# A decoder layer on one core: inverse and pair products by chunks of 64, another order of the expert loads, and another last pair

## The reference

```python
# gated DeltaNet, 4 heads, chunks of C = 64 tokens
L = where(strict, einsum("bhncd,bhnmd->bhncm", kb, k) * decay, 0)   # per chunk, C x C
T = triangular_solve(L + eye, eye)                                  # inverse, per chunk
u = T @ vb;  w = T @ (kb * exp(gc))
attn = where(incl, einsum("bhncd,bhnmd->bhncm", q, k) * decay, 0)
...   # a scan over the chunks, forgetting attention, gates, output projection, router
# experts: 32, 4 per token
gu = xb @ w_gate_up[e] + b_gate_up[e]                # 1024 x 2048 weights
act = (clip(up) + 1) * (gate * sigmoid(1.702 * gate))
y = act @ w_down[e] + b_down[e]                      # 1024 x 1024 weights
x = x + gt2 * sum of y by gates;  return rms_norm(x, g_final)
```

## Time and profile before

| | us |
|---|---|
| three runs | 1253.33, 1255.08, 1256.19 |
| median | 1255.08 |
| the profiled execution | 1258.74 |
| its span | 1256.7 |
| PE busy | 1152.5 (92%) |
| DVE, ACT, POOL busy | 322.5, 185.2, 106.0 |
| mean rate of all transfers | 370 GB/s |

### The profile page before, as it was taken

One profiled execution on the slowest core, in us unless ns is written; L12 is line 12 of the kernel. 1 busy time (PEld: TensorE's weight loads), 2 busy tenths in 40 slices (PEclk: granted clock), 3 DMA queues, 4 the chain that ended last, 5 costly groups with the idle time before them and its releaser, 6 DMA issues.

```text
span 1256.7 us, 14765 instructions
## 1 busy us (share of the span) xinstructions
PE 1152.5 (92%) x6083; PEld 601.5 (48%) x6083; DVE 322.5 (26%) x674; ACT 185.2 (15%) x316; POOL 106.0 (8%) x50
## 2 busy tenths in 40 slices
PE   4999999999999999998988989898999999999995
PEld 2999799778634434333333333333333333343431
DVE  1633554132232222212221212122121222222112
ACT  2475244100301000000000000000000010000001
POOL 0764343020000000000000000000000000000000
PEclk9999999999999999999999999999999999999998
DMA  9972763398789999999999999999999999999994
GB/s 350 340 231 90 231 217 101 102 414 371 291 363 424 428 428 429 429 428 428 429 428 428 430 427 429 430 427 429 429 428 430 428 428 421 386 429 429 428 426 176
DMA packets 62268, 464.67 MB, mean 370 GB/s; under 512 B 8437, under 2 KB 31098, under 8 KB 34586
## 3 DMA queue, kind: packets, MB, share of 16 engines
q1 hardware_dynamic: 60968, 462.13, 89.6%
q10 hardware_dynamic: 1218, 1.93, 0.5%
q0 software_dynamic: 48, 0.13, 0.0%
HBM read 463.13 MB, written 1.05 MB: 369 GB/s over the span
## 4 chain that ended last, share of the span: by engine, by line
PE 67%; DMA 26%; issue 3%; ACT 2%; DVE 1%; ACTq 0%; SPq 0%; DVEq 0%
PE ps L438 65%; DMA ring<-in_w_down_dram 22%; DMA ring<-in_w_gate_up_dram 3%; PE ps L871 1%; ACT kept L1195 1%; DMA ring<-in_w_in_dram 1%; DMA ring<-in_g_onorm_dram 1%; PE ps L893 0%; PE ps L446 0%; ACT w_hi L1003 0%; DVE ring L1662 0%; ACT ring L986 0%; DVE kept L1326 0%; ACT ring L1041 0%; ACT ring L1212 0%
## 5 line engine op out<-in xcount | busy, mean ns | idle before, releaser
L438 PE MATMUL ps<-ring,kept 128*64 128x512 f32 (+1 forms) x3280 | 713.7, 602 | 44.1 <-DMA ring<-in_w_down_dram 32.5
L438 PEld LDWEIGHTS ps<-ring,kept 128*64 128x64 f32 (+1 forms) x3280 | 230.9, 138 | 496.4 <-issue 428.7
L438 PE MATMUL ps<-kept 128*128 128x128 f32 (+5 forms) x744 | 139.2, 350 | 5.5 <-DVE kept L1564 1.6
L1191 ACT ACTIVATE kept<-kept 128x512 f32<-128x512 f32 x32 | 20.2, 630 | 746.3 <-DVE kept L1598 746.3
L1617 DVE TENSOR_TENSOR kept<-ps,kept 64x512 f32<-64x512 f32 x64 | 44.1, 689 | 315.9 <-PE ps L438 314.9
L438 PEld LDWEIGHTS ps<-kept 128*128 128x128 f32 (+2 forms) x744 | 94.1, 192 | 58.7 <-issue 53.2
L1598 DVE TENSOR_SCALAR kept<-ps 128x512 f32<-128x512 f32 x32 | 22.1, 691 | 371.2 <-PE ps L438 371.2
L1674 POOL TENSOR_TENSOR w_lo<-ring,w_hi 128x1024 fp32r<-128x1024 f32 x38 | 91.9, 2435 | 116.7 <-ACT w_hi L1003 116.7
L438 PE MATMUL ps<-ring 128*128 128x128 f32 (+4 forms) x560 | 87.1, 314 | 2.4 <-issue 2.4
L438 PEld LDWEIGHTS ps<-ring 128*128 128x128 f32 (+3 forms) x560 | 78.4, 193 | 11.0 <-issue 6.3
L438 PE MATMUL ps<-hT_hi,w_hi 128*128 128x256 f32 x272 | 78.4, 288 | 0.0
(11 more groups left out here) (227 smaller groups left out, 519.4 us busy)
## 6 DMA issues: line engine op xcount, KB each, us to landing
ring<-in_w_gate_up_dram SPq DMA_DIRECT2D x128, 2048.0 KB, 26.9
ring<-in_w_down_dram SPq DMA_DIRECT2D x63, 2048.0 KB, 23.8
ring<-in_w_ada_dram SPq DMA_DIRECT2D x24, 1024.0 KB, 5.4
ring<-in_w_in_dram SPq DMA_DIRECT2D x22, 1024.0 KB, 11.4
ring<-in_w_out_dram SPq DMA_DIRECT2D x4, 1024.0 KB, 15.7
ring<-in_w_o_fox_dram SPq DMA_DIRECT2D x2, 1024.0 KB, 9.8
ring<-in_w_o_delta_dram SPq DMA_DIRECT2D x2, 1024.0 KB, 12.2
kept<-in_w_down_dram SPq DMA_DIRECT2D x1, 2048.0 KB, 14.1
```

Source lines behind the costliest of these rows:

```text
L438: return pe.matmul(dst, lhsT, rhs, start=start, stop=stop, skip_group_check=True)
L1191: A(sig_a, gate_a, ACT.Sigmoid, scale=ALPHA).then_inc(S("sig_ready"), 1)
```

## The change

Four parts. (1) The pair products, and the products of the inverse but for R and XR of level 1, are done per chunk: for each `t` and `h` two multiplications, one per chunk `r`. In the pair products each has 128 rows, 64 stationary columns and 64 moving ones; in the inverse each is a 64x64 tile on the diagonal of the array by 64 columns. (2) The transposes of the gate weights go from the start of `open_sums` into the first gate_up, ahead of row block 6. (3) Down weights have three places: low halves of even experts in units 16 and 17, low halves of odd ones in `dn_kept` (the place of `early_dn`), high halves of both in units 18 and 19. The order of the loads is `by_place` for pairs 1 to 9, a mixed one for pair `TURN` = 10, `by_need` for 11 to 14. The very first unit of pair 1 comes as two loads of one row block each, the first of which waits for one used row block instead of two. (4) The last pair has both gate_ups ahead of both downs, in its loads and on TensorE. The even expert's transposed activations go to a place of their own (`act_t_last`), VectorE's steps follow (`last_experts`), and the high half of the last down comes as two loads of 1 MB into units 4 and 5.

```diff
-            def load_dn(e, j):
-                src = w_down[0, e, j * 4 * P:(j + 1) * 4 * P, :].rearrange("(p k) n -> p (k n)", k=4)
-                s0 = 16 + 2 * j
-                sp.dma_start(flat[:, s0 * UNIT:(s0 + 2) * UNIT], src).then_inc(expert_chunk_sem(s0), 16)
+            def load_gu_row(e, par, u, k):
+                src = w_gate_up[0, e, u * 2 * P:(u + 1) * 2 * P, :].rearrange("(p k) n -> p k n", k=2)
+                s0 = par * KD + 2 * u
+                sp.dma_start(flat[:, (s0 + k) * UNIT:(s0 + k + 1) * UNIT], src[:, k, :]).then_inc(
+                    expert_chunk_sem(s0), 16)
+            def dn_rows(e, j):
+                return w_down[0, e, j * 4 * P:(j + 1) * 4 * P, :].rearrange("(p k) n -> p (k n)", k=4)
+            def load_dn(e, par, j):
+                if j == 1:
+                    sp.dma_start(flat[:, 18 * UNIT:20 * UNIT], dn_rows(e, 1)).then_inc(S("dn_high_in"), 16)
+                elif par == 0:
+                    sp.dma_start(flat[:, 16 * UNIT:18 * UNIT], dn_rows(e, 0)).then_inc(S("dn_even_in"), 16)
+                else:
+                    sp.dma_start(dn_kept, dn_rows(e, 0)).then_inc(S("dn_odd_in"), 16)
...
-            def next_dn(I, i, par, js=range(2)):
-                for j in js:
-                    sp.wait_ge(S("dn_used"), I * 8 + (par * 4 - 4 + 2 * j + 2))
-                    load_dn(i * 2 + par, j)
+            def next_dn(I, i, par, j):
+                if j == 1:
+                    sp.wait_ge(S("dn_used"), I * 8 + par * 4)
+                else:
+                    sp.wait_ge(S("dn_used"), I * 8 + (par * 4 - 6))
+                load_dn(i * 2 + par, par, j)
+            def by_place(I, i, first_unit_whole=True):
+                if first_unit_whole:
+                    next_gu(I, i, 0)
+                else:
+                    for k in range(2):
+                        sp.wait_ge(S("gu_used"), I * 16 + (k - 15))
+                        load_gu_row(i * 2, 0, 0, k)
+                    next_gu(I, i, 0, range(1, 4))
+                next_dn(I, i, 0, 0)
+                next_dn(I - 1, i - 1, 1, 1)
+                next_gu(I, i, 1)
+                next_dn(I, i, 1, 0)
+                next_dn(I, i, 0, 1)
+            def by_need(I, i):
+                for par in range(2):
+                    next_gu(I, i, par)
+                    for j in range(2):
+                        next_dn(I, i, par, j)
+            def last_by_need(I, i):
+                for par in range(2):
+                    next_gu(I, i, par)
+                for j in range(2):
+                    next_dn(I, i, 0, j)
+                next_dn(I, i, 1, 0)
+                sp.wait_ge(S("gu_used"), I * 16 + 6)
+                rows = w_down[0, i * 2 + 1, 4 * P:8 * P, :].rearrange("(p k) n -> p k n", k=4)
+                for half, sem in enumerate((S("dn_last_in0"), S("dn_last_in1"))):
+                    at = 4 * UNIT + half * UNIT
+                    sp.dma_start(flat[:, at:at + UNIT].rearrange("p (k n) -> p k n", k=2),
+                                 rows[:, 2 * half:2 * half + 2, :]).then_inc(sem, 16)
             def load_round(I0, first):
-                if not first:
+                if first:
+                    by_place(1, 1, first_unit_whole=False)
+                else:
+                    sp.wait_ge(S("dn_used"), I0 * 8)
                     next_gu(I0, 0, 0)
-                    next_dn(I0, 0, 0)
+                    next_dn(I0, 0, 0, 0)
+                    next_dn(I0, 0, 0, 1)
                     next_gu(I0, 0, 1)
-                if first:
-                    next_gu(I0 + 1, 1, 0)
-                    next_dn(I0, 0, 1, range(1, 2))
-                    next_gu(I0 + 1, 1, 1)
-                    next_dn(I0 + 1, 1, 0)
-                with sp.Fori(2 if first else 1, PAIRS - 3) as i:
-                    next_gu(I0 + i, i, 0)
-                    next_dn(I0 + (i - 1), i - 1, 1)
-                    next_gu(I0 + i, i, 1)
-                    next_dn(I0 + i, i, 0)
-                i = PAIRS - 3
-                next_gu(I0 + i, i, 0, range(1))
-                next_dn(I0 + (i - 1), i - 1, 1)
-                next_gu(I0 + i, i, 0, range(1, 4))
-                next_dn(I0 + i, i, 0)
-                next_gu(I0 + i, i, 1)
-                next_dn(I0 + i, i, 1)
-                for i in (PAIRS - 2, PAIRS - 1):
-                    for par in range(2):
-                        next_gu(I0 + i, i, par)
-                        next_dn(I0 + i, i, par)
+                    next_dn(I0, 0, 1, 0)
+                with sp.Fori(2 if first else 1, TURN) as i:
+                    by_place(I0 + i, i)
+                next_gu(I0 + TURN, TURN, 0)
+                next_dn(I0 + TURN, TURN, 0, 0)
+                next_dn(I0 + (TURN - 1), TURN - 1, 1, 1)
+                next_gu(I0 + TURN, TURN, 1, range(0, 2))
+                next_dn(I0 + TURN, TURN, 0, 1)
+                next_gu(I0 + TURN, TURN, 1, range(2, 4))
+                next_dn(I0 + TURN, TURN, 1, 0)
+                next_dn(I0 + TURN, TURN, 1, 1)
+                with sp.Fori(TURN + 1, PAIRS - 1) as i:
+                    by_need(I0 + i, i)
+                last_by_need(I0 + (PAIRS - 1), PAIRS - 1)
...
+            def chunk_products(banks, a, b):
+                for t in range(TT):
+                    for h in range(H):
+                        for r in range(2):
+                            rows = slice(r * CH, r * CH + CH)
+                            last = mm(ps[rows, banks[t], h * P + r * CH:h * P + r * CH + CH], a[rows, t, h, rows],
+                                      b[rows, t, h, rows], True, True)
+                return last
+            def chunk_pairs(banks, a, b):
+                for t in range(TT):
+                    for h in range(H):
+                        for r in range(2):
+                            rows = slice(r * CH, r * CH + CH)
+                            toks = slice(t * P + r * CH, t * P + r * CH + CH)
+                            last = mm(ps[rows, banks[t], h * P + r * CH:h * P + r * CH + CH], a[:, h, toks],
+                                      b[:, h, toks], True, True)
+                return last
             nproj = [0]
@@ -608,18 +686,10 @@
             project("z", 1)
             pe.wait_ge(S("tok_taken"), 1)
-            for t in range(TT):
-                for h in range(H):
-                    a = kn[:, h, t * P:(t + 1) * P]
-                    last = mm(bank((2, 7)[t], h * P, P), a, a, True, True)
-            last.then_inc(S("pairs_ps"), 1)
+            chunk_pairs((2, 7), kn, kn).then_inc(S("pairs_ps"), 1)
...
-                for t in range(TT):
-                    for h in range(H):
-                        last = mm(bank((2, 7)[t], h * P, P), Mm[:, t, h, :], Um[:, t, h, :], True, True)
-                last.then_inc(S("R_ps"), 1)
+                (whole_products if s == 1 else chunk_products)((2, 7), Mm, Um).then_inc(S("R_ps"), 1)
...
-                for t in range(TT):
-                    for h in range(H):
-                        last = mm(bank(5 + t, h * P, P), Xm[:, t, h, :], Rm[:, t, h, :], True, True)
-                last.then_inc(S("XR_ps"), 1)
+                (whole_products if s == 1 else chunk_products)((5, 6), Xm, Rm).then_inc(S("XR_ps"), 1)
...
-                    for t in range(TT):
-                        for h in range(H):
-                            last = mm(bank(3 + t, h * P, P), Rm[:, t, h, :], Xm[:, t, h, :], True, True)
-                    last.then_inc(S("RX_ps"), 1)
+                    chunk_products((3, 4), Rm, Xm).then_inc(S("RX_ps"), 1)
...
-            def gate_up(i, par, first=False):
+            def gate_up(i, par, first=False, opening=False):
+                extra = 16 if par == 0 and not opening else 0
                 for k in range(KD):
                     if first and k == 4:
                         pe.wait_ge(S("xg_high_ready"), i + 1)
+                    if opening and k == 6:
+                        open_transposes()
                     if k % 2 == 0:
-                        pe.wait_ge(expert_chunk_sem(par * KD + k), i * 16 + (16 + STREAMED[par * KD + k]))
+                        pe.wait_ge(expert_chunk_sem(par * KD + k),
+                                   i * 16 + (16 + STREAMED[par * KD + k] + (extra if k == 0 else 0)))
                     for q in range(4):
...
-            def down(i, par, early=False):
+            def down(i, par, high, js=range(2), acts=None, last_of=None):
                 e = i * 2 + par
-                pe.wait_ge(S("act_t_ready"), e + 1)
-                for k in range(KD):
+                acts = act_t if acts is None else acts
+                if js[0] == 0:
+                    pe.wait_ge(S("act_t_ready"), e + 1)
+                for k in range(4 * js[0], 4 * js[-1] + 4):
                     j, kk = k // 4, k % 4
-                    if kk == 0:
-                        pe.wait_ge(expert_chunk_sem(16 + 2 * j), i * 32 + (par * 16 + 16))
```

(73 more changed lines are left out.)

58 lines of the change are left out of this document (29 added, 29 removed).

## The result

| | before | after |
|---|---|---|
| median of 4 runs, us | 1255.63 (1253.33 to 1256.63) | 1238.96 (1238.21 to 1241.62) |
| profiled execution, us | 1258.74 | 1238.21 |
| its span, us | 1256.7 | 1236.4 |

The ratio is 0.9874 (95% interval 0.9853 to 0.9895): 16.7 us faster by the medians, 20.3 by the two profiled spans. The forecast was 1233.7 in a range of 1228 to 1246, 21.4 us faster. The profile follows part by part.

What follows compares the result with a forecast made beforehand. After about 330 us the expert weight stream was taken to set the pace. Gains of 10.0 + 5.1 + 0.4 + 5.9 = 21.4 us off the 1255.08 us median gave 1233.7 us, range 1228 to 1246.

Steps and rivals of the forecast that it cites:

- turn: At pair 10, where the load order switches: 3.3 us of stream lost instead of 3.7, a gain of 0.4 us.
- first load earlier: Front of the kernel: products by chunks let the expert weight stream start 10.0 us earlier.
- first holes: Stream gaps at 336 to 340 and 358 to 366 us: 2.1 us lost instead of 7.2, gaining 5.1.
- tail: Last pair: last down ends 2.4 us after the last landing instead of 8.3, gaining 5.9 us.
- Groups: Fourteen product groups in pair products and inverse: 0.89 us instead of 1.78 each, as halves run side by side; 12.5 saved.
- (a): Rival, chance 0.21: the inverse's diagonal tiles don't run side by side, the front gains nothing, 1243.7 us.
- (d): Rival, chance 0.08: small diagonal records run in turn with weight loads exposed; slower above 0.085 us a record, up to 1275.
- Tile changes: Switching tile shape around 10 runs of groups: 20 changes at 0.09 us each, costing 1.8 us.
- The 0.7 for VectorE: Inverse levels: 0.7 us taken off the front's gain because VectorE's work barely fits the shorter levels.
- (c): Rival, chance 0.07: VectorE or GpSimd's weight split limits the shorter levels, half the front gain lost, 1239 us.
- (e): Rival, chance 0.06: load order does nothing, holes stay, only front and tail count, 1239 us.
- (b): Rival, chance 0.08: TensorE slows at each pair's long wait; turn and tail lose some 3 us each, holes partly reappear; 1240.

Runs made afterwards that it cites:

- before_again: The kernel before, unchanged, profiled a second time: 1253.21 us (1 run), span 1251.2 us.
- tiles_in_turn: The kernel after, but each inverse group issues all upper-chunk records first, then all lower ones: 1247.0 us, ratio 0.9935 to the kernel before.
- last_pair_old: The kernel after, but with the last pair's loads and engine work in the old order: 1244.28 us, ratio 0.9911 to the kernel before.
- filled_twice: The kernel after with two gate_up units of pair 11 each loaded ahead of a waiting high down half: 1232.81 us, ratio 0.9829 to the kernel before.
- no_products: The kernel after with all products whole 128x128 again: 1247.16 us, ratio 0.9928 to the kernel before.
- turn_filled: The kernel after with pair 11's first gate_up unit loaded ahead of pair 10's odd high down half: 1237.71 us, ratio 0.9866 to the kernel before.

## Why the prediction was right, and where its terms were off

The direction and the range held, and so did the mechanism, but for the turn; the gain was 16.7 instead of 21.4 us. Term by term, against each of the two profiles of the kernel before:

| | forecast | from the profile of before | from before_again | by medians |
|---|---|---|---|---|
| first load earlier | 10.0 | 9.1 | 6.5 | 8.2 |
| first holes | 5.1 | 7.4 - 0.8 = 6.6 | 5.6 - 0.8 = 4.8 | |
| turn | 0.4 | 3.6 - 4.3 = -0.7 | 3.5 - 4.3 = -0.8 | |
| tail | 5.9 | 8.3 - 2.4 = 5.9 | 7.0 - 2.4 = 4.6 | 5.3 |
| sum | 21.4 | 20.9 | 15.1 | 16.7 |
| spans | | 20.3 | 14.8 | |

(The 6.5 has the projection fast in before_again and slow in after; with those 1.7 us it is 8.2. The 7.0: last gate_up there at 1222.48, landing 9.8 later, down over at 1230.53 + 8.78.) Holes and turn by medians are what is left, 16.7 - 8.2 - 5.3 = 3.2, with an uncertainty of some us: against the kernel before beside each run the 8.2 is 9.6 and the 5.3 is 6.7. The sums close within 0.6 us of the spans, so no further cause is needed.

1. **Groups.** Forecast 0.89 us saved each, 12.5 in all; a group adds 0.93 instead of 1.78, so 0.85 are saved, 11.9 in all. Right, and rivals (a) and (d) fall with it: tiles_in_turn shows that the diagonal tiles of a pair do run side by side. (The threshold of (d), 0.085 us a record, leaves out the 1.4 us of the pairs that it names; with them it is 0.089. Both are far from 0.029.)
2. **Tile changes.** The mis-sized term of the front. The forecast read 0.09 us for one change off, which is an entry, and took it for leaving too. A run of groups between half projections costs 0.34 in and out together. Over all ten runs the cost is smaller than ten times that, since some are followed by other shapes: the stretch of 107.30 us fell by 8.6, or by 9.0 without the longer wait of point 3, so they cost 11.9 - 9.0 = 2.9 instead of 1.8.
3. **The 0.7 for VectorE.** No wait of TensorE for VectorE stands inside the levels. Rival (c) falls. Instead up to 1.0 us went into two longer waits further on: for the modulation rows 1.24 us (before 0.82) and ahead of the projection 2.99 (before 2.44). The second is partly scatter, since it is 2.48 to 2.99 in the profiles with the new products and 2.44 to 2.69 in those with the whole ones. 11.9 - 2.9 - 1.0 = 8.0, and the runs gave 7.0 and 8.2.
4. **First holes.** 2.1 us forecast to remain, 0.8 did. That only 4.8 were won and not 5.1 is due to the base: the 7.2 us of the earlier trace rows stood in a profile whose slow gather delayed the places. Rival (e) falls.
5. **The loop by places.** No hole, and one long wait per pair: right, but for two places where three waits follow each other half a pair apart. The long ones last 3.1 to 3.5 us, not 5.
6. **The turn.** The forecast of 3.3 us lost was 1.5 and some 2 for TensorE being slower behind its one wait, as in rival (b). 4.3 were lost; the gain of 0.4 became a loss of 0.7. The place is as forecast, the odd high half waiting for the even down, but that the number came near is luck. TensorE was slower behind the wait (5.13 us for the half at 859.97) and had made it up: the even down of pair 10 starts at 911.73, 51.8 us after that landing, forecast 51.6. The 1.5 was what was too small. It took the landing of the last unit, 58.8 us on, as the moment at which the stream runs dry, and that unit does land 58.7 on, at 918.6; but in windows of 0.5 us the rate falls from 426 to 131 GB/s at 915.5 already. And the new load landed 7.7 us after its issue, not 1.65 + 4.9 = 6.6. The rest of (b), holes coming back and a slow tail, didn't come.
7. **The tail.** As forecast to the tenth in the profile (2.4 after the last landing), and by the path forecast: the last down starts 4.7 us ahead of the last landing, behind VectorE. By last_pair_old it is worth 5.3, since the old tail is 7.0 to 8.3.
8. **The base.** The sum was taken off a profiled execution with several slow stretches, and its terms were applied to the median. Part of what the change "removed" in that profile is not there in most runs. With 8.2 and 5.3 by medians, the miss of 4.7 us is 1.8 in the front, 1.1 at the turn, 0.3 in the first holes and 0.6 in the tail, which make 3.8; the rest is within the scatter of the medians.

What stays open: why the clock falls at the projection in one profile and not in another. The length of the wait doesn't tell them apart (2.48 us and slow in filled_twice, 2.69 and fast in no_products). The slow halves in the loop by places weren't tried for themselves either, as the stream hides them.

## What to carry to other kernels

Where the stream of loads sets the pace, look for the few moments at which it runs dry and for the load that ends each: a hole at a place-bound load is filled by letting a load whose place is free flow first, and then the same question comes up one step later (turn_filled moved the hole, filled_twice removed it). Reckon such a hole by landings: a load of 2 MB on a queue that has run dry landed 7.7 us after its issue here, against 4.9 from unit to unit. Small block-diagonal products on TensorE pay if the records of the two halves alternate and if the groups stand together, since every run among whole-array work costs some 0.34 us. Before terms are read off one profile, see whether it lies at the median; if the same instructions stand with two durations in it, take the base from a second one.

## What the runs showed of the hardware

- Diagonal 64x64 tiles that alternate run two at a time even into one PSUM bank: 0.029 us a record, 0.05 in turn.
- A run of small tiles between whole-array records costs 0.34 us beyond its own records, and only 0.09 of it lie ahead of its first record. The weight loads go with the 0.10 by which the second record afterwards is late; view of the weight loads of TensorE in the kernel after:

```profile
178.27 0.19 PEld L488 LDWEIGHTS ps<-hT_hi,w_hi 128*128 128x128 f32 x1
178.37 0.19 PEld L488 LDWEIGHTS ps<-hT_lo,w_hi 128*128 128x128 f32 x1
178.49 0.19 PEld L488 LDWEIGHTS ps<-hT_hi,w_lo 128*128 128x128 f32 x1
```

The load at 178.27 begins together with its matmul, which lasts 0.39 us instead of 0.28; from the next on a load is one record ahead.

- TensorE is slower behind some waits of 2.4 to 3.5 us, and sometimes behind one of 0.98 (the gather). Windows of 4 us in the kernel after (the column before the last two is the granted clock, as a share of 2.4 GHz):

```profile
564.00:568.00 4.00, 1.67 (x4) 0.53 (x6) 0.00 (x0) 0.00 (x0) 0.00 (x0) 0.75 1.01 430
568.00:572.00 4.00, 4.00 (x18) 1.29 (x16) 0.44 (x1) 0.00 (x0) 0.00 (x0) 0.82 1.00 426
```

The shares of 0.75 and 0.82 mean that a part of each window ran at 1.2 GHz and the rest at 2.4. The same instructions took 3.69 or 5.38 us at the projection, and 3.81 or 5.44 at the gather, from one execution to the next; two such places explain several us between runs of one kernel.
